# Recurrence decay by an exponential on ScalarE, with all four recurrence blocks scanned before the sequential attention

## The reference

```python
def rg_lru(x, w_rg, b_rg, w_ig, b_ig, lam):
    r = sigmoid(block_diag_linear(x, w_rg, b_rg))
    i = sigmoid(block_diag_linear(x, w_ig, b_ig))
    log_a = -8.0 * r * softplus(-lam)
    a = exp(log_a)
    mult = sqrt(-expm1(2.0 * log_a))
    bterm = mult * (i * x)
    # h[t] = a[t] * h[t-1] + bterm[t], along the 512 tokens
    return associative_scan(combine, (a, bterm))
...
# second block, simplified
u = rms_norm(x) @ w_in                       # lru_x, lru_g, q, k, v
hl = rg_lru(conv4(lru_x), ...)               # 512 channels = 4 blocks of 128
y_lru = gelu(lru_g) * hl
y_att = stick_breaking_attention(q, k, v)    # 8 heads, 4 query blocks
x = x + concat(rms_norm(y_lru), rms_norm(y_att)) @ w_out
x = x + (silu(h2 @ w_gate) * (h2 @ w_up)) @ w_down
```

## Time and profile before

| | before |
|---|---|
| runs (us) | 1379.61, 1380.45, 1381.43 |
| median (us) | 1380.45 |
| span of the profiled execution (us) | 1377.8 |
| PE busy | 1335.7 us, 97% |
| DVE busy | 787.6 us, 57% |
| POOL busy | 611.5 us, 44% |
| ACT busy | 550.0 us, 40% |
| mean granted TensorE clock | 0.992 of full |

### The profile page before, as it was taken

The page is one execution under the profiler, slowest core; times in us unless marked ns, Lnnn a source line. Parts: engine busy times, 40 slices in busy tenths (PEclk is TensorE's granted clock), DMA queues, the critical chain, the costliest instruction groups (busy, mean ns, idle before and its releaser), DMA issues. The chain is left out here.

```text
span 1377.8 us, 18053 instructions
## 1 busy us (share of the span) xinstructions
PE 1335.7 (97%) x6189; PEld 1083.1 (79%) x6189; DVE 787.6 (57%) x1097; ACT 550.0 (40%) x860; POOL 611.5 (44%) x299
## 2 busy tenths in 40 slices
PE   8998989999999999999999999899999999999997
PEld 7787767887678888888888777678688888888887
DVE  7788896642457777777434588765543333332231
ACT  5444676542353233232232354545443223223322
POOL 4597873332244444444434533122244444444441
PEclk9999999999999999999999999999999999999999
DMA  6122320221122232233232222011122222233222
GB/s 229 60 92 92 108 78 31 92 78 61 46 92 92 91 105 93 91 105 102 98 105 86 86 80 87 31 54 54 59 86 101 91 100 98 91 100 106 101 86 81
DMA packets 31875, 121.19 MB, mean 88 GB/s; under 512 B 3536, under 2 KB 3664, under 8 KB 31568
## 3 DMA queue, kind: packets, MB, share of 16 engines
q1 hardware_dynamic: 31536, 119.81, 25.7%
q10 hardware_dynamic: 288, 0.69, 0.1%
HBM read 118.40 MB, written 2.10 MB: 87 GB/s over the span
## 5 line engine op out<-in xcount | busy, mean ns | idle before, releaser
L619 POOL TENSOR_TENSOR weights_low<-weights_raw,weights_high 128x1024 fp32r<-128x1024 f32 (+1 forms) x204 | 525.8, 2578 | 733.1 <-ACT weights_high L697 732.9
L697 ACT CAST weights_high<-weights_raw 128x1024 fp32r<-128x1024 f32 (+1 forms) x202 | 222.0, 1099 | 506.7 <-PE acc L1730 474.3
L1730 PE MATMUL acc<-a_high,weights_high 128*128 128x512 f32 x976 | 389.6, 399 | 1.8 <-DVE a_low L1392 1.1
L1730 PE MATMUL acc<-a_high,weights_low 128*128 128x512 f32 x976 | 380.9, 390 | 0.0
L1730 PE MATMUL acc<-a_low,weights_high 128*128 128x512 f32 x976 | 380.4, 390 | 0.0
L1730 PEld LDWEIGHTS acc<-a_high,weights_high 128*128 128x128 f32 x976 | 183.5, 188 | 44.2 <-issue 3.8
L1730 PEld LDWEIGHTS acc<-a_low,weights_high 128*128 128x128 f32 x976 | 183.6, 188 | 39.0 <-issue 2.6
L1730 PEld LDWEIGHTS acc<-a_high,weights_low 128*128 128x128 f32 x976 | 183.3, 188 | 38.8
L1202 DVE TENSOR_TENSOR residual<-acc,residual 128x512 f32<-128x512 f32 (+1 forms) x63 | 43.3, 687 | 174.3 <-PE acc L1730 129.8
L1730 PE MATMUL acc<-h_high,weights_high 128*128 128x512 f32 x330 | 129.1, 391 | 0.0
L1730 PE MATMUL acc<-h_high,weights_low 128*128 128x512 f32 x330 | 128.6, 390 | 0.0
(11 more groups left out here) (384 smaller groups left out, 1955.4 us busy)
## 6 DMA issues: line engine op xcount, KB each, us to landing
weights_raw<-w SPq DMA_DIRECT2D x172, 512.0 KB, 3.2
weights_raw<-w SPq DMA_DIRECT2D x32, 704.0 KB, 4.0
residual<-xT SPq DMA_DIRECT2D x8, 256.0 KB, 6.7
out<-y_tok SPq DMA_DIRECT2D x4, 512.0 KB, 3.1
mem_raw<-memT SPq DMA_DIRECT2D x1, 1024.0 KB, 5.3
mem_tok<-mem SPq DMA_DIRECT2D x1, 1024.0 KB, 7.4
lru_weights<-blockdiag ACTq DMA_DIRECT2D x1, 512.0 KB, 3.3
sine<-positions SPq DMA_DIRECT2D x1, 256.0 KB, 7.3
```

What stands on the lines that cost most here:

```text
L619: g.tensor_tensor(weights_low[:, s, 0:cols], weights_raw[:, s, 0:cols], weights_high[:, s, 0:cols].bitcast(F32), ALU.subtract).then_inc(we ...
L697: a.copy(weights_high[:, s, 0:cols], weights_raw[:, s, 0:cols]).then_inc(weight_high, 1)
L1730: last = t_.matmul(acc[:, bank, 0:cols], w[:, s, wide], x_[:, k0 + k, 0:cols], start=start and k == opens and n == 0, stop=stop and k == c ...
```

## The change

The decay a is now made by ACT as exp(-2 d r), where r is the recurrence gate and d the per-channel factor (`decay`). DVE's pass for 1 + t, its reciprocal and the pass 2 / (1 + t) - 1 go. The factor of the scan's input is (1 + a) sqrt(t), which is the same number. The sigmoid r is kept in the new tile `keep`, one per block, and the exponential overwrites it there. A small DVE instruction makes `decay_twice` once. ACT has one more table of functions to load, for the exponential, so its batches "keep", "root" and "gelu" now stand behind tiles 6, 7 and 8, where "root" and "gelu" stood behind tiles 6 and 7. All four "late" items stand ahead of step 0.

```diff
-        REC_PLAN += pieces(6) + [("root", j) for j in range(4)] + [("inverse", 1), ("late", 0)]
...
+        REC_PLAN += pieces(6) + [("keep", j) for j in range(4)]
+        REC_PLAN += pieces(7) + [("root", j) for j in range(4)] + [("late", 0)]
+        REC_PLAN += pieces(8) + [("gelu", j) for j in range(4)] + [("late", 1)]
+        REC_PLAN += pieces(9) + [("turn", 0), ("late", 2)] + pieces(10) + [("late", 3)]
...
-        AFTER = {0: [("late", 2)], 1: [("hidden", 0)], 2: [("late", 3)], 3: [("hidden", 1), ("square", 0)],
+        AFTER = {1: [("hidden", 0)], 3: [("hidden", 1), ("square", 0)],
...
                     act.wait_ge(lgates_done, 2 * j + r + 1)
-                    if j:
-                        act.wait_ge((tanh_ready, gated_in)[r], j)
-                    a.activation(gates[:, r], aux[2 + (2 * j + r) % 4][:], ACT.Sigmoid,
+                    if r and j:
+                        act.wait_ge(gated_in, j)
+                    a.activation(gates[:] if r else keep[:, j], aux[2 + (2 * j + r) % 4][:], ACT.Sigmoid,
                                  bias=col(("b_rg", "b_ig")[r], j)).then_inc(lgates_ready, 1)
...
+                elif what == "keep":
+                    act.wait_ge(tanh_ready, j + 1)
+                    act.wait_ge(decay_ready, 1)
+                    a.activation(keep[:, j], keep[:, j], ACT.Exp, scale=decay_twice[:, j:j + 1]
+                                 ).then_inc(keep_ready, 1)
...
+            v.tensor_scalar(decay_twice, decay, -2.0, None, ALU.mult).then_inc(decay_ready, 1)
...
                 elif what == "before":
-                    dve.wait_ge(tanh_ready, j + 1)
-                    v.tensor_scalar(inverse_sum[:, j], body, 1.0, None, ALU.add).then_inc(tanh_used, 1)
                     dve.wait_ge(lgates_ready, 2 * j + 2)
-                    v.tensor_tensor(xc[:, j], gates[:, 1], xc[:, j], ALU.mult).then_inc(gated_in, 1)
-                elif what == "inverse":
-                    dve.wait_ge(tanh_used, j + 1)
-                    own.then(v.reciprocal(inverse_sum[:, j], inverse_sum[:, j]))
+                    v.tensor_tensor(xc[:, j], gates[:], xc[:, j], ALU.mult).then_inc(gated_in, 1)
                 elif what == "late":
                     dve.wait_ge(lroot_ready, j + 1)
                     dve.wait_ge(gated_in, j + 1)
-                    own.then(v.scalar_tensor_tensor(body, body, 2.0, inverse_sum[:, j], ALU.mult, ALU.mult))
-                    own.step(v.tensor_tensor(xc[:, j], body, xc[:, j], ALU.mult))
-                    own.then(v.tensor_scalar(inverse_sum[:, j], inverse_sum[:, j], 2.0, -1.0, ALU.mult,
-                                             ALU.add))
-
-                    v.tensor_tensor_scan(body, inverse_sum[:, j], xc[:, j], 0.0, ALU.mult, ALU.add
+                    dve.wait_ge(keep_ready, j + 1)
+                    own.then(v.scalar_tensor_tensor(body, keep[:, j], 1.0, body, ALU.add, ALU.mult))
+                    own.then(v.tensor_tensor(xc[:, j], body, xc[:, j], ALU.mult))
+                    v.tensor_tensor_scan(body, keep[:, j], xc[:, j], 0.0, ALU.mult, ALU.add
                                          ).then_inc(lru_done, 1)
```

15 lines of the change are left out of this document (7 added, 8 removed).

## The result

| | before | after |
|---|---|---|
| median (us) | 1380.94 (1379.61 to 1382.19) | 1372.42 (1371.07 to 1373.43) |
| ratio of the times | | 0.9941 [0.9929, 0.9952] |
| profiled execution, span (us) | 1377.8 | 1371.0 (its time 1372.86) |
| PE busy (us) | 1335.7 | 1331.5 |
| DVE busy (us) | 787.6 | 771.1 |

The change makes the kernel 0.6% faster, 8.5 us by these medians and 6.6 to 9.8 us by the interval. The prediction said 1374.7 us and a range from 1373.4. With only four executions of each kernel here, the 8.5 us is the largest gain of any group of runs: over all runs of this document the median of before is 1380.2 us (73 executions) and that of after 1372.9 (10 executions), 7.3 us apart.

A forecast was written before the change was run, and what follows sets the result against it. PE, busy 97% of the span, was taken as the bound; terms of 6.2 us at the `square_sum` matmuls less 0.4 left 5.8, so span 1377.8 became 1372.0, plus 2.65 gave 1374.7 us, range 1373.4 to 1378.0.

The forecast's parts named there:

- gap 1: PE's idle time before the transposes of attention step 1, forecast to go: 1.77 us.
- gap 2: PE's idle time in attention step 7, behind a late DVE `take`, forecast to go: 0.27 us.
- the forecast stands to the median as the sum to the span: Step from profiled span to time: 2.65 us added around the span of 1372.0, giving 1374.7 us.
- gap 3: PE's 2.58 us idle before step 8, forecast to shrink to 0.87: 1.71 us.
- clock: Half clock on PE's matmuls behind the wait before step 8, forecast to stay at 2.4 GHz instead: 1.37 us counted.
- gap 4: PE's idle time before the sum over `square_sum`, forecast to go: 0.81 us plus a tail of 0.25, 1.06 us.
- table loads ahead of the spread: ACT's root and sigmoid table loads behind the `square_sum` matmuls, forecast to make the spread late: -0.4 us.
- some 3 us for each of the blocks: DVE work of recurrence blocks 2 and 3 leaving attention steps 0 to 7, forecast as what pays.
- rival B: Last addition to `square_sum` lands behind POOL's subtraction again: 1376.7 us, or 1378.1 with half clock; chance 0.20.
- C: ACT's squares still delay the copy of q before step 8: only 2.9 us gained, 1377.5 us; chance 0.12.
- D: Attention starts late because blocks 2 and 3 precede its first scan: slower, 1381.5 us or more; chance 0.03.
- better than A: A gain above the forecast 5.8 us, with the clock also spared elsewhere; chance 0.05.

The follow-up runs named there:

- place_only: Kernel before with only the recurrence blocks 2 and 3 moved ahead of step 0, decay still on DVE: 1374.89 us, ratio 0.9962.
- math_only: Changed kernel with the exponential decay kept but blocks 2 and 3 back behind steps 0 and 2: 1381.22 us, ratio 1.0000 to before.
- late_behind_1: Kernel before with recurrence block 2 moved behind step 1 of the attention, block 3 still behind step 2: 1379.02 us, ratio 0.9994.
- a_again: The changed kernel, unchanged, run and profiled again: 1372.94 us, ratio 0.9950 to before.
- a_third: The changed kernel, unchanged, one more execution for a third profile: 1373.33 us.
- b_again: The kernel before, unchanged, run and profiled again: 1380.41 us, ratio 1.0002.
- gaps_filled: Kernel before with 15 unread PE matmuls added, 10 ahead of step 8 and 5 behind it: 1379.45 us, ratio 0.9993.
- b_third: The kernel before, unchanged, one more execution for a third profile: 1381.0 us.
- tighter: Changed kernel with out-projection chunk tile by tile, pieces ahead of steps 8, 16, 24, earlier head-pair copies, spread one step later: 1365.41 us, ratio 0.9889.

## Why the prediction was off, and what it had right

The measured 1372.42 us lies below the stated range. The mechanism was the forecast one, and the failure is in sizes, at two steps. The sum took the idle time in PE's row for the whole of a wait, so that gaps 1 and 2 and what lies between them stood with 2.04 us and gave 2.64. And "the forecast stands to the median as the sum to the span" carried over to the changed kernel 0.8 us that the median of before has on top of the execution that I read, and that the changed kernel doesn't have.

**Right: where the time was, and what would free it.** The gain is PE's arrival at the sum, and it came at the places named. The last column is the matched starts.

| term | forecast | measured |
|---|---|---|
| gap 1, transposes of step 1 | 1.77 | 1.94 |
| from there to step 6 | not named | 0.22 |
| gap 2, step 7 | 0.27 | 0.48 |
| gap 3, step 8 (0.87 to remain, 0.88 did) | 1.71 | 1.76 |
| clock and gap 4 together | 2.43 | 2.33 |
| table loads ahead of the spread | -0.4 | -0.26 |
| sum | 5.8 | 6.47 |

`place_only` and `math_only` show that it is the place of the blocks 2 and 3 that pays, as the forecast said of "some 3 us for each of the blocks". In `late_behind_1` moving one of them within the steps doesn't.

**Right: the added work is hidden.** An exponential takes 0.64 us, where the forecast had 0.65. All three table loads take 1.28 us, with the activation 0.01 to 0.02 us behind them. The drain of 1.38 us on each switch that the Trainium skill's page "ScalarE: Activation LUTs" (section "What ACT_TABLE_LOAD costs") has on top of the load isn't seen in this kernel; by it the time would have been nearer 1376.2. The casts came 0.4 to 0.5 us earlier with the whole execution, not later.

**Right by a hair: rival B.** The forecast gave the last addition a margin of 0.4 us over POOL's subtraction. It was 0.13 us (0.12 in each of `a_again` and `a_third`), in an either-or that the forecast priced at 2.0 us. The section "SBUF: two separate sides" of the Trainium skill's page "SBUF — State Buffer" has whoever starts first keep the shared ports for the whole instruction, and both orders were seen: DVE's operations of 0.4 to 0.7 us took 2.1 to 2.6, and POOL's of 2.4 took 2.81 and 3.36. The rivals C and D didn't come about in the changed kernel; the mechanism of D did in `place_only`, with 1.6 us.

**Wrong: the step from the span to the time.** The forecast said "As 1377.8 + 2.65 is by construction the median, the forecast stands to the median as the sum to the span". That put 2.65 us around a span, from a median and another execution's span. Where a run gives both numbers, what lies around is 1.8 to 2.1 us (1372.86 - 1371.0, 1379.26 - 1377.3, 1381.0 - 1379.0). The execution that I read was thus one of about 1379.7 us, 0.8 under its median of 1380.45 and 0.5 under the 1380.2 of all executions. The kernel before does spend these 0.8 us in its median execution, but not in the gaps that I added up, and the forecast let the changed kernel spend them too. It doesn't: the execution of after that I read (1372.86) is at the median of all ten (1372.9). A part of the difference is seen in `b_again`: 1.2 us for a half clock behind the wait, in a stage where the changed kernel has none. How often the kernel before pays that isn't shown.

**Wrong by a size: the waits before the transposes, 0.6 us too small.** At gap 4 I had counted 0.25 us for a matmul whose modelled end reaches into the wait; at gaps 1 and 2 I took the idle time as it stood in PE's row. There it hides 0.17 and 0.21 us, and 0.22 us between the two don't show in it at all. The weight loads (PEld) show such waits, in the kernel before:

```profile
848.21 0.14 PEld L2122 LDWEIGHTS aux<-ident,take 128*128 128x128 f32 x1 [2.10 <-DVE take L1581]
...
859.56 0.31 PEld L2122 LDWEIGHTS aux<-ident,take 128*128 128x128 f32 x3 [0.41 <-DVE take L1581]
...
863.12 0.31 PEld L2122 LDWEIGHTS aux<-ident,take 128*128 128x128 f32 x3 [0.81 <-DVE take L1581]
```

PE's row has 1.77 and 0.27 us of idle where PEld's has 2.10 and 0.81, and at 859.56 PEld waits 0.41 us for DVE where PE's row has none at all. After the change PEld still waits 0.33 us in each of the steps 6 and 7, in step 7 not for DVE. The differences, 0.08 and 0.48, are what the matched starts gained at those two places. In step 3 PEld's wait fell by 0.14 us more (0.37 to 0.23). The Trainium skill's "Perfetto Trace Analysis", section "Tensor Engine Instruction (MATMUL, LD_WEIGHTS)", says that a matmul's end is worked out and not observed, and these rows agree.

**Right in the sum, wrong in the reason: the clock.** The forecast made the half clock a term of its own, 1.37 us, and said that it "needn't be in every run: without it 4.4 us are left". `gaps_filled` and `b_again` refute that: without half clock in that place PE just waits longer for the addition, and the 2.4 us are DVE's either way. What the clock adds is what falls behind the wait, 0 in two profiles of before and 1.2 us in the third. The rival "better than A" named the clock, but not as a cost that comes and goes in the kernel before.

**The balance.** 1374.65 - 1372.42 = 2.2 us. Of these 0.8 are the time around the span, 0.7 the stage's terms (6.47 against 5.78), 0.3 the two executions' difference outside of the stage, and 0.4 that the read execution of after was 0.44 us above the median of its group. The last two are scatter that I haven't explained further than by where the half clock fell. The low end of 1373.4 stood 1.3 us below the forecast, and the first two alone are 1.5. In the later groups after came out at 1372.94 and, in a single execution, 1373.33, with 1380.28 and 1379.81 for before. These too lie below the range, by 0.5 and 0.1 us.

## What to carry to other kernels

A pass that is taken off an engine on which nothing waits pays only when the work behind it moves out of the place where another engine does wait: here the cheaper decay gave nothing measurable and the move 5.4 us, and together they gave 7.3. When a wait and a slow stretch end at the same releaser they are one term, so ask for each what else arrives at that moment. Take the time around the span from an execution that gives both numbers, and read a small wait of PE in its weight loads as well as in its matmuls.

## What the runs showed of the hardware

- A DVE reciprocal of 128x512 (3.33 us at 837.71 in `place_only`) runs beside a POOL subtraction that starts at 838.85 and takes its usual 2.41 us. Neither holds the other. DVE passes with two SBUF inputs are held: 2.42 us for the scan at 844.87 in the same kernel, which reads `stay` twice. The prediction's "DVE instructions whose inputs lie in SBUF wait for a subtraction that is under way" is too wide.
- POOL's subtraction waits in its turn: 2.81 us where DVE's addition was 0.13 us ahead, 3.36 us where a scan of 1.22 us was.
- The half clock (granted clock 0.50 to 0.51) at a gap of the same 2.57 or 2.58 us started within 0.5 us of the gap's end in three profiles (0.5 before it in before and `b_third`, 0.3 behind it in `math_only`) and 5.7 us later in the fourth (`b_again`, 867.75 to 873.5), and lasted 3.4 us in three and 10.2 in `math_only`. The length of the gap alone doesn't decide: 3.19 us in `late_behind_1` (before 857.56) and 3.21 us in `tighter` (before 877.66) were followed by no half clock for 15 us. The changed kernel's gaps of up to 1.17 us between 863 and 928 us never brought it.
